# Expert weights in a ring of 22 pieces of 1 MB instead of 11 slots of 2 MB

## The reference

```python
def moe_ffn(h, expert, gate, w_gate, w_up, w_down):
...
    def expert_block(args):
        xblk, e = args
        return (jax.nn.silu(xblk @ w_gate[e]) * (xblk @ w_up[e])) @ w_down[e]
```

## Time and profile before

| what | value |
|---|---|
| three runs, median (lowest to highest) | 2089.93 us (2085.76 to 2095.61) |
| the profiled execution: time, span | 2090.83 us, 2089.1 us |
| mean granted TensorE clock | 0.934 |
| busy share PE, DVE, ACT, POOL | 85%, 37%, 20%, 14% |
| HBM read | 759.10 MB, 364 GB/s over the span |
| `in_w_gate`, `in_w_up`, `in_w_down` | 64 transfers of 2048 KB each |

### The profile page before, as it was taken

One profiled execution on the slowest core, in us unless ns is written; L12 is line 12 of the kernel. 1 busy time (PEld: TensorE's weight loads), 2 busy tenths in 40 slices (PEclk: granted clock), 3 DMA queues, 4 the chain that ended last, 5 costly groups with the idle time before them and its releaser, 6 DMA issues. The chain is left out here.

```text
span 2089.1 us, 23422 instructions
## 1 busy us (share of the span) xinstructions
PE 1768.7 (85%) x9328; PEld 914.3 (44%) x9328; DVE 771.6 (37%) x1877; ACT 423.4 (20%) x990; POOL 299.1 (14%) x284
## 2 busy tenths in 40 slices
PE   9999986886766555668999999888799999998886
PEld 7779862553321111124554444233377544442332
DVE  3955176776667777854230000000213300000002
ACT  2481122221222112223121010000123201110001
POOL 0000033453334444440000000000000000000000
PEclk9999998998886876689999999999999999999999
DMA  7236279999999999997789999999944999999996
GB/s 262 93 131 290 101 299 388 409 415 422 422 421 421 421 421 421 421 420 302 292 360 428 426 428 427 426 426 426 423 181 187 412 427 426 427 427 427 427 426 277
DMA packets 78973, 761.80 MB, mean 365 GB/s; under 512 B 8628, under 2 KB 9621, under 8 KB 17542
## 3 DMA queue, kind: packets, MB, share of 16 engines
q1 hardware_dynamic: 41190, 489.34, 56.1%
q0 software_dynamic: 37664, 270.84, 31.5%
HBM read 759.10 MB, written 1.05 MB: 364 GB/s over the span
## 5 line engine op out<-in xcount | busy, mean ns | idle before, releaser
L2584 PE MATMUL bank<-arena 128*64 128x512 f32 x3072 | 684.3, 599 | 55.3 <-DMA arena<-in_w_up 19.6
L1057 PE MATMUL bank<-arena 64*64 64x512 f32 x2032 | 324.6, 794 | 233.7 <-ACT arena L772 233.6
L2584 PEld LDWEIGHTS bank<-arena 128*64 128x64 f32 x3072 | 233.8, 138 | 492.0 <-issue 470.8
L563 POOL DMA_INDIRECT arena<-in_peer_uv,arena x256 | 287.4, 1123 | 631.5 <-PE bank L1057 305.9
L1401 DVE CUSTOM_DVE_ANT_0 arena<-arena 128x1024 f32<-128x1024 f32 x256 | 313.6, 1225 | 171.2 <-DMA arena<-in_peer_uv,arena 168.0
L1057 PEld LDWEIGHTS bank<-arena 64*64 64x64 f32 x2032 | 93.9, 177 | 444.8 <-ACT arena L772 265.7
L2711 DVE TENSOR_TENSOR arena<-arena,bank 128x512 f32<-128x512 f32 x32 | 22.0, 687 | 718.5 <-PE bank L2584 718.5
L822 PE MATMUL bank<-arena 128*128 128x272 f32 (+2 forms) x768 | 145.2, 349 | 0.5 <-ACT arena L596 0.3
L822 PEld LDWEIGHTS bank<-arena 128*128 128x128 f32 x768 | 126.4, 191 | 19.9 <-issue 2.5
L767 ACT ACTIVATE arena<-arena 128x4 f32<-128x4 f32 (+1 forms) x65 | 13.3, 205 | 466.4 <-DVE arena L1401 466.4
L1487 POOL DMA_DIRECT2D arena<-in_w_router x2 | 1.1, 574 | 562.4 <-POOLq L2469 528.0
(11 more groups left out here) (444 smaller groups left out, 1482.9 us busy)
## 6 DMA issues: line engine op xcount, KB each, us to landing
arena<-in_w_up SPq DMA_DIRECT2D x64, 2048.0 KB, 36.9
arena<-in_w_gate SPq DMA_DIRECT2D x64, 2048.0 KB, 32.9
arena<-in_w_down SPq DMA_DIRECT2D x64, 2048.0 KB, 39.0
arena<-in_w_in SPq DMA_DIRECT2D x13, 2048.0 KB, 8.5
arena<-in_w_out SPq DMA_DIRECT2D x2, 4096.0 KB, 17.9
arena<-in_wq SPq DMA_DIRECT2D x4, 2048.0 KB, 13.6
arena<-in_rg_out SPq DMA_DIRECT2D x1, 4096.0 KB, 13.9
arena<-in_peer_uv,arena POOLq DMA_INDIRECT x256, 17.4
```

The source lines that it names most:

```text
L563: nc.gpsimd.indirect_dma_start(SLOT[slot_of[j]], None, d["peer_uv"], bass.IndirectOffsetOnAxis(IDX[:, u % 4, k:k + 1], 0)).then_inc(s_row[ ...
L1057: m = pe.matmul(bank[banks[t][half]][to:to + HALF, :], DIAG[lo:lo + HALF, k + j, :], row[lo:lo + HALF, D + half * 512:D + (half + 1) * 512 ...
L2584: x = pe.matmul(bank[b][j * C:(j + 1) * C, :], operand[:, c, j * C:(j + 1) * C], RING[s % AHEAD][:, c % (DC // 2), j, :], start=(c == 0), ...
```

## The change

A slot's 16 KB runs are cut in two runs of 8 KB. The ring keeps its 11 slots of memory and their addresses, but they are treated as 22 pieces of 1 MB; `moe_load` issues one piece, each piece has a semaphore of its own, TensorE waits for a piece before its matmuls (8 in the profile) and releases it after them, and SP waits for the release of a piece before it loads it anew. A pair of experts is 24 pieces. All counts of `s_step` in the waits of the other engines are doubled, so that they wait for the same matmuls as before; so are the waits ahead of the layer norm's and the attention weights.

The 22 semaphores are one set for both layers. Twelve of them are semaphores of the front stage that are used a second time (its weights' own, `K.s_front_w`); POOL clears these at the start of the gating stage and all 22 at the start of the dilated stage, and SP waits in both stages for the router's first constant (`s_cst` at 1), which POOL makes behind the clears, before it issues the first expert piece.

```diff
--- before.py
+++ after.py
@@ -426,12 +426,12 @@
...
-    s_x, s_cols, s_idft, s_gw, s_rgo, s_hyo, s_wo = (sem("mix_" + n) for n in (
-        "x_in", "cols_in", "idft_in", "gatew_in", "rgout_in", "hyout_in", "wout_in"))
-    s_ring = [sem(f"mix_ring{k}_in") for k in range(2)]
+    s_x, s_cols, s_idft = (sem("mix_" + n) for n in ("x_in", "cols_in", "idft_in"))
+    s_gw, s_rgo, s_hyo, s_wo = (K.lasting_sem(n + "_then_expert_weights_in") for n in ("gatew", "rgout", "hyout", "wout"))
+    s_ring = [K.lasting_sem(f"projection_then_expert_weights{k}_in") for k in range(2)]
...
-    s_meta, s_first = sem("mix_meta_in"), sem("mix_first_weights_in")
+    s_meta, s_first = K.lasting_sem("meta_then_expert_weights_in"), K.lasting_sem("first_then_expert_weights_in")
...
@@ -446,7 +446,8 @@
...
-    s_wq = [sem(f"peer_wq{k}_in") for k in range(4)]
+    s_wq = [K.lasting_sem(f"query_then_expert_weights{k}_in") for k in range(4)]
+    K.s_front_w = s_wq + s_ring + [s_meta, s_first, s_hyo, s_rgo, s_wo, s_gw]
...
@@ -1670,7 +1671,7 @@
...
-    K.s_moe_w = [K.lasting_sem(f"moe0_w{i}_in") for i in range(MOE_SLOTS)]
+    K.s_moe_w = K.s_front_w + [K.lasting_sem(f"moe_w{i}_in") for i in range(RING_PIECES - len(K.s_front_w))]
...
@@ -1704,8 +1705,10 @@
 
             def experts(*slots):
                 for i in slots:
-                    moe_load(K, sp, 0, i, 0).then_inc(K.s_moe_w[i], 16)
-
+                    for piece in (2 * i, 2 * i + 1):
+                        moe_load(K, sp, 0, piece, 0).then_inc(K.s_moe_w[piece], 16)
+
+            sp.wait_ge(router.s_cst, 1)
             experts(4)
             sp.wait_ge(s_gm, len(GATED))
             experts(5)
@@ -1722,6 +1725,8 @@
         def _(pool):
             router.gpsimd_loads(pool)
             K.clear_stale(pool)
+            for s in K.s_front_w:
+                pool.sem_clear(s)
             router.gpsimd(pool, nc.gpsimd, K.IOTA)
...
@@ -1997,8 +2002,6 @@
...
-    K.s_moe_w = [K.lasting_sem(f"moe1_w{i}_in") for i in range(MOE_SLOTS)]
...
@@ -2045,9 +2048,11 @@
 
             def experts(*slots):
                 for i in slots:
-                    moe_load(K, sp, 1, i, 0).then_inc(K.s_moe_w[i], 16)
+                    for piece in (2 * i, 2 * i + 1):
+                        moe_load(K, sp, 1, piece, 0).then_inc(K.s_moe_w[piece], 16)
 
             sp.wait_ge(s_pm, VALUE_JOBS)
+            sp.wait_ge(router.s_cst, 1)
             experts(9)
             sp.wait_ge(s_pm, job("k", DPAIRS - 1) + 1)
@@ -2065,6 +2070,8 @@
         def _(pool):
             router.gpsimd_loads(pool)
             K.clear_stale(pool)
+            for s in K.s_moe_w:
+                pool.sem_clear(s)
             router.gpsimd(pool, nc.gpsimd, K.IOTA)
@@ -2361,7 +2368,8 @@
 MOE_SLOTS = 11
 EARLY_SLOTS = 10
 PASSES = 2 * T // P
-HALVES = 2 * len(MOE_STEPS)
+PIECES = 4 * len(MOE_STEPS)
+RING_PIECES = 2 * MOE_SLOTS
 
 
 def moe_base(K, slots):
@@ -2369,16 +2377,17 @@
     return K.cols - slots * DC * 512
 
 
-def moe_slot(K, i):
-
-    return K.cut(moe_base(K, i + 1), P, DC // 2, 2, 512)
+def moe_piece(K, s):
+
+    return K.cut(moe_base(K, s // 2 + 1) + s % 2 * DC * 256, P, DC // 4, 2, 512)
 
 
 def moe_load(K, sp, layer, i, pair):
 
-    name, h = MOE_STEPS[i // 2]
-    src = K.dram[name][layer * NE + pair * 2 + h:layer * NE + pair * 2 + h + 1, :, i % 2, :]
-    return sp.dma_start(moe_slot(K, (pair * HALVES + i) % MOE_SLOTS), src.rearrange("o p (c j n) -> p (o c) j n", j=2, n=512))
+    name, h = MOE_STEPS[i // 4]
+    src = K.dram[name][layer * NE + pair * 2 + h:layer * NE + pair * 2 + h + 1, :, i // 2 % 2, :]
+    src = src.rearrange("o p (c j n) -> p (o c) j n", j=2, n=512)
+    return sp.dma_start(moe_piece(K, (pair * PIECES + i) % RING_PIECES), src[:, i % 2 * (DC // 4):(i % 2 + 1) * (DC // 4)])
@@ -2398,11 +2407,11 @@
     PAIRS = NE // 2
     STEPS = MOE_STEPS
     NS = len(STEPS)
-    AHEAD = MOE_SLOTS
-    LAPS = [len(range(k, PAIRS * HALVES, AHEAD)) for k in range(AHEAD)]
-
-    at = Room(moe_base(K, AHEAD), ROUTE_COLS + 2 * T + 2 * MEM_W)
-    RING = [moe_slot(K, i) for i in range(AHEAD)]
+    AHEAD = RING_PIECES
+    LAPS = [len(range(k, PAIRS * PIECES, AHEAD)) for k in range(AHEAD)]
...
@@ -2420,7 +2429,7 @@
-    FIRST_FREE = PAIRS * HALVES - (AHEAD - 2)
+    FIRST_FREE = PAIRS * PIECES - 2 * (MOE_SLOTS - 2)
...
@@ -2470,25 +2479,25 @@
         @block.sync
         def _(sp):
             def load(q, e):
-                for i in range(EARLY_SLOTS if isinstance(q, int) and e == 0 else 0, HALVES):
-                    s = e * HALVES + i
+                for i in range(2 * EARLY_SLOTS if isinstance(q, int) and e == 0 else 0, PIECES):
+                    s = e * PIECES + i
                     if isinstance(q, int) and s < AHEAD:
                         moe_load(K, sp, layer, i, e).then_inc(s_w[s], 16)
                         continue
-                    used = s - AHEAD if s >= AHEAD else s + (LAPS[s] - 1) * AHEAD - PAIRS * HALVES
-                    since(sp, s_step, q * (PAIRS * HALVES) + (used + 1))
+                    used = s - AHEAD if s >= AHEAD else s + (LAPS[s] - 1) * AHEAD - PAIRS * PIECES
+                    since(sp, s_step, q * (PAIRS * PIECES) + (used + 1))
                     moe_load(K, sp, layer, i, e).then_inc(s_w[s % AHEAD], 16)
 
             visits(sp, load)
             more = sp.value_load(K.NMORE[0:1, 0:1], min_val=0, max_val=PASSES - 1)
 
-            sp.wait_ge(s_step, more * (PAIRS * HALVES) + (PAIRS * HALVES - (AHEAD - 3)))
+            sp.wait_ge(s_step, more * (PAIRS * PIECES) + (PAIRS * PIECES - 2 * (MOE_SLOTS - 3)))
             sp.dma_start(LG, d["ln2_g"][layer].partition_broadcast(P)).then_inc(s_par, 16)
             sp.dma_start(LB, d["ln2_b"][layer].partition_broadcast(P)).then_inc(s_par, 16)
             if not last_layer:
-                steps = sp.value_load(NSTEPS[0:1, 0:1], min_val=FIRST_FREE, max_val=FIRST_FREE + (PASSES - 1) * (PAIRS * HALVES))
+                steps = sp.value_load(NSTEPS[0:1, 0:1], min_val=FIRST_FREE, max_val=FIRST_FREE + (PASSES - 1) * (PAIRS * PIECES))
                 names = ("w_v", "w_k", "w_in1")
-                for n, (to, name, later) in enumerate(zip(dilated_weights(K), names, (0, 3, 5))):
+                for n, (to, name, later) in enumerate(zip(dilated_weights(K), names, (0, 6, 10))):
...
@@ -2520,7 +2529,7 @@
...
-                    act.wait_ge(s_step, n * HALVES + (2 * b + 2))
+                    act.wait_ge(s_step, n * PIECES + (4 * b + 4))
...
@@ -2529,7 +2538,7 @@
...
-                    act.wait_ge(s_step, n * HALVES + (2 * b + 10))
+                    act.wait_ge(s_step, n * PIECES + (4 * b + 20))
...
@@ -2576,14 +2585,15 @@
             def step(q, e, i, operand, b, s_op, used, part=range(DC)):
 
                 for c in part:
-                    s = e * HALVES + 2 * i + c // (DC // 2)
+                    s = e * PIECES + 4 * i + c // (DC // 4)
                     if c % (DC // 2) == 0:
                         te.wait_ge(s_op, used + (c // (DC // 2) + 1))
+                    if c % (DC // 4) == 0:
                         te.wait_ge(s_w[s % AHEAD], q * (LAPS[s % AHEAD] * 16) + (s // AHEAD * 16 + 16))
                     for j in range(2):
                         x = pe.matmul(bank[b][j * C:(j + 1) * C, :], operand[:, c, j * C:(j + 1) * C],
-                                      RING[s % AHEAD][:, c % (DC // 2), j, :], start=(c == 0), stop=(c == DC - 1))
-                    if c % (DC // 2) == DC // 2 - 1:
+                                      RING[s % AHEAD][:, c % (DC // 4), j, :], start=(c == 0), stop=(c == DC - 1))
+                    if c % (DC // 4) == DC // 4 - 1:
                         x.then_inc(s_step, 1)
...
@@ -2689,7 +2699,7 @@
...
-                do(v.tensor_scalar(NSTEPS, NPF, float(PAIRS * HALVES), float(PAIRS * HALVES - FIRST_FREE), ALU.mult, ALU.subtract))
+                do(v.tensor_scalar(NSTEPS, NPF, float(PAIRS * PIECES), float(PAIRS * PIECES - FIRST_FREE), ALU.mult, ALU.subtract))
...
@@ -2705,7 +2715,7 @@
...
-                    ve.wait_ge(s_step, n * HALVES + (2 * b + 6))
+                    ve.wait_ge(s_step, n * PIECES + (4 * b + 12))
...
```

More of the change, by code:

```diff
@@ L2400, in moe_stage @@
     NS = len(STEPS)
-    AHEAD = MOE_SLOTS
-    LAPS = [len(range(k, PAIRS * HALVES, AHEAD)) for k in range(AHEAD)]
-    at = Room(moe_base(K, AHEAD), ROUTE_COLS + 2 * T + 2 * MEM_W)
-    RING = [moe_slot(K, i) for i in range(AHEAD)]
+    AHEAD = RING_PIECES
+    LAPS = [len(range(k, PAIRS * PIECES, AHEAD)) for k in range(AHEAD)]
+    at = Room(moe_base(K, MOE_SLOTS), ROUTE_COLS + 2 * T + 2 * MEM_W)
+    RING = [moe_piece(K, i) for i in range(AHEAD)]
     XE = cut(at.take(DC * P), P, DC, P)
@@ L2412, in moe_stage @@
     Y_BANKS = ((4, 5), (6, 7))
-    after = Room(moe_base(K, AHEAD - 1), moe_base(K, AHEAD))
+    after = Room(moe_base(K, MOE_SLOTS - 1), moe_base(K, MOE_SLOTS))
     LB, LG = (cut(after.take(D), P, D) for _ in range(2))
```

## The result

The changed kernel takes 2100.3 us in the median of 9 runs (2096.5 to 2106.2), the kernel before 2090.6 us in 9 runs, the three above among them. The ratio is **1.0036, 95% interval 1.0025 to 1.0048**: some 7.5 us slower (5.2 to 10.0; the two medians are 9.7 us apart), within the half per cent that was called "same", and inside the range. The sign is nevertheless resolved: it is a small loss, three times the +2.3 us that the sum gave.

What follows compares the result with a forecast made beforehand. DMA was taken to bound both expert stages: bytes over rate plus start and tail. Terms +9.0 +0.5 -1.8 -0.6 -1.8 -3.0 = +2.3 us on 2090.8, median 0.9 lower, so 2092 us; range 2083 less 1 to 2104.

Steps and rivals of the forecast that it cites:

- What bounds: In both expert stages DMA bounds: start of the gapless stream, bytes over rate, then TensorE's work after the last landing.
- Rate of the stream: In both expert streams, 8 KB runs lower 426.6 GB/s to 422: +4.5 us a stage, +9.0 in all.
- Start of the stream: At each expert stage's start, the first release comes 1.8 us earlier: -1.8 and -0.6 us; slower early loads +0.5.
- Tail: At each expert stage's end, half slots land earlier and are worked through meanwhile: -1.8 and -3.0 us.
- Issues and waits: 192 more SP issues at 0.33 us each and 192 more TensorE waits cost nothing.
- Semaphores: POOL's added clears in the gating and dilated stages and SP's wait for the first constant cost nothing.
- Runs cost nothing: Rival, chance 0.22: expert streams stay at 426.6 GB/s, gains of 7.2 us remain, 2083 us.
- The gains don't come: Rival, chance 0.10: the slowest DMA engine sets landings, so starts and tail give nothing; +9.5 us, 2100 us.
- The 8 KB packet is dear: Rival, chance 0.16: expert streams at 417.8 GB/s or below, slower by over half a per cent; at 415, 2106 us.

Runs made afterwards that it cites:

- the tail alone: Kernel before with only slots 94 and 95 of each layer loaded in two halves, with a wait for each: 2088.5 us, ratio 0.9979.
- the experiment made for it: Kernel before with each slot in two 1 MB transfers keeping 16 KB runs, partitions 0 to 63 and 64 to 127: 2881, 2907, 2983 and 2986 us.

## Why the prediction was right, and where its sum was off

**What bounds** (right): bytes over rate. Every kernel above moved by its stream's rate and its tail, and the chain kept its 51.0 us.

**Rate of the stream** (mis-sized, the step that carries the error). The prediction took 422 GB/s and +9.0 us; the trace gives 419.5 and +14.0, and the 8 KB run alone, with the slots untouched, +16.1 (13.4 to 18.6). It stayed within the bounds of 0 to 17.2, but 419.5 lies below the 420 to 424 that the forecast named. The error came from choosing a value between the gathers at 421 and a line through two microseconds of 4 KB rows. Those rows gave 418; a whole stream of them gives 409. A window of 2 us with 204 packets should have set a bound and not been half of the estimate; the gathers were nearer, 1.5 GB/s too high. The rule of the Trainium skill weighed there, 3 cycles per packet ("DMA: Bandwidth & Descriptors", section "Why small descriptors are slow"), was still further off: it gives 0.6% where 1.6% to 1.7% were measured. The 341 GB/s for 1 MB, in the section "Bandwidth" of the same page of the Trainium skill, is not what these transfers, queued one behind the other, reach: they move at 419.5.

**Start of the stream** (wrong, the gain did not come). Predicted -1.8 and -0.6, with +0.5 for the early loads, -1.9 in all; from slot 10's issue to slot 94 the changed kernel takes 7.0 us more a stage, all of which is its rate, so the start is worth nothing. The issue that comes 1.7 us earlier does not by itself shorten the stage: slot 12's release stays where it is. The prediction followed one gap to its end and did not ask what is late next.

**Tail** (right in mechanism, one term taken from a chance event). 7.44 us in both stages was computed as 7.4 to 8.3. But 1.7 of the 3.0 us in the second stage stood against a matmul row at a granted clock of 0.66 that the other executions with whole slots do not have. The typical gain is 9.15 - 7.44, twice: -3.4 and not -4.8 (in two stages of other executions TensorE waited for slot 95 too, and the tail was 9.5 and 9.9 us, so it can be half a microsecond more); the tail alone measured -4.4 (-2.3 to -6.5), which does not tell the two apart.

**Issues and waits** (right that they cost nothing, wrong in the reason for SP). "0.33 us each" was the free issue; with 22 pieces SP is held for 2.14 us in most of them. Nothing else is queued there, so it is harmless.

**Semaphores** (right): 1.0001.

Put together from the traces: +14.0 + 0 - 3.4 = **+10.6 us**, against 7.5 (5.2 to 10.0) measured, and medians 9.7 and, the second time, 5.9 us apart. That is just above the interval; the rest of some 3 us is not explained. The three terms erred the same way, by 5.0, 1.9 and 1.4 us. The total stayed in the range because the bounds of the rate were wide, and the mechanism that it rests on, bytes over rate plus a tail, is what the runs show.

Of the rivals, "Runs cost nothing" fell at 420 GB/s; its hope that halved waits keep the clock up in the tail is not borne out by the 3.63 us above. "The gains don't come" fell with the tail and held for the start. "The 8 KB packet is dear" was nearer than the forecast's centre: 419.5 is 1.7 GB/s from its threshold of 417.8.

What stays open is whether 1 MB transfers cost a little beside their shorter runs: 419.5 against 419.9 is all that the traces show, and the experiment made for it measured something else. Open too is what the 8 KB runs alone lose beyond their rate: 16.1 us were measured (13.4 to 18.6), of which 419.9 GB/s accounts for 13.3.

## What to carry to other kernels

Where a stream of transfers is the bound, read its rate per packet and not per transfer: compare windows of hundreds of microseconds at two run lengths, take the fixed price from them, and multiply. Split only the transfers whose granularity sets an end, here the last two slots, and leave the body of the stream in the longest runs that the buffers hold. Make the body longer where one engine can still catch up, and stop the long ones early enough that it does.

## What the runs showed of the hardware

- A packet from DRAM to this memory costs an engine 8 to 10 ns beside its bytes at 4, 8 and 16 KB (160.2, 312.2, 614.5 ns). At 8 KB it made little difference whether the transfer had 1 or 2 MB (419.5 and 419.9 GB/s). With 32 KB runs in most of the stream the rate rises further, to 430 GB/s.
- SP's queue takes only so much and then holds SP inside the issue (2.14 us in the median with 1 MB in 8 KB runs, 0.33 where nothing is held). In flight, by landing time over time per transfer: 10.7 transfers of 1 MB in 8 KB runs (26.7/2.50), 6.5 of 2 MB in 8 KB runs (32.6/4.99), 4.6 of 2 MB in 4 KB runs (23.8/5.13). Per engine that is 96, 111 and 153 packets, so the limit is neither a number of transfers nor one of packets; it was not found.
- Two transfers of 1 MB to 64 adjacent partitions each, issued one behind the other, together need about twice the time of one of 2 MB to 128: 224 against 427 GB/s.
